# A decoder layer on one core: LN2's gain and bias rows made by TensorE transposes, a 1 MB weight load moved ahead, and one 4 MB piece loaded in two transfers instead of four

## The reference, cut to what matters

```python
h = layer_norm(ALPHA*h + hybrid_mixer(h, ...), ln1_g, ln1_b)
h = layer_norm(ALPHA*h + memory_cross_attention(h, mem_n, ...), ln2_g, ln2_b)     # LN2
# router: top 4 of 32 experts per token, softmax weights -> combine
for e in range(32):
    hid = clamped_swiglu(h @ w_mlp1[e] + b_mlp1[e])      # w_mlp1[e]: 1024 x 2048, 8 MB
    y   = y + combine[:, e:e+1] * (hid @ w_mlp2[e] + b_mlp2[e])   # w_mlp2[e]: 1024 x 1024, 4 MB
h = layer_norm(ALPHA*h + y, ln3_g, ln3_b)
```

## Time and profile before

| | |
|---|---|
| runs | 1135.2, 1135.61, 1135.63 us; median 1135.61 |
| profiled execution | 1137.09 us, of which the profiled span is 1135.2 us |
| busy in the span | PE 1084.9, PEld 522.0, DVE 322.2, ACT 228.6, POOL 8.1 us |
| transfers | 446.74 MB (here of 10^6 bytes) in all, mean 394 GB/s over the span |
| granted TensorE clock | mean 0.99 |

### The profile page before, as it was taken

The page is one execution under the profiler, slowest core; times in us unless marked ns, Lnnn a source line. Parts: engine busy times, 40 slices in busy tenths (PEclk is TensorE's granted clock), DMA queues, the critical chain, the costliest instruction groups (busy, mean ns, idle before and its releaser), DMA issues.

```text
span 1135.2 us, 15726 instructions
## 1 busy us (share of the span) xinstructions
PE 1084.9 (96%) x6536; PEld 522.0 (46%) x6536; DVE 322.2 (28%) x733; ACT 228.6 (20%) x411; POOL 8.1 (1%) x14
## 2 busy tenths in 40 slices
PE   9999999989999999999999999999999999999996
PEld 6888899843333333343333333333333333334331
DVE  6987775581111111121111111111111111012112
ACT  5667565440000100010010000000000000001001
POOL 0000000000000000000000000000000000000000
PEclk9999999999999999999999999999999999999999
DMA  9866868699999999999999999999999999999996
GB/s 354 295 193 238 289 209 331 230 388 419 436 431 435 432 433 432 435 433 433 432 434 434 432 435 433 433 432 435 433 432 433 434 434 431 431 430 429 432 426 250
DMA packets 41728, 446.74 MB, mean 394 GB/s; under 512 B 4832, under 2 KB 5728, under 8 KB 25088
## 3 DMA queue, kind: packets, MB, share of 16 engines
q1 hardware_dynamic: 41408, 445.76, 94.0%
q10 hardware_dynamic: 288, 0.52, 0.1%
HBM read 445.22 MB, written 1.05 MB: 393 GB/s over the span
## 4 chain that ended last, share of the span: by engine, by line
PE 58%; DMA 35%; SPq 3%; DVE 3%; issue 1%; ACT 0%; DVEq 0%
DMA ring<-in_w_mlp 33%; PE bank L1155 23%; PE bank L1199 9%; PE bank L685 5%; PE bank L687 5%; PE bank L686 5%; PE bank L1057 4%; PE bank L1045 2%; DMA w_raw<-in_w_in 2%; SPq L609 1%; PE bank L1094 1%; SPq L488 1%; SPq L502 1%; PE bank L927 1%; PE bank L911 1%; PE bank L1113 1%
## 5 line engine op out<-in xcount | busy, mean ns | idle before, releaser
L1155 PE MATMUL bank<-ring,live 128*64 128x512 f32 x2048 | 468.2, 605 | 27.9 <-DMA ring<-in_w_mlp 27.7
L1155 PEld LDWEIGHTS bank<-ring,live 128*64 128x64 f32 x2048 | 143.8, 138 | 310.4 <-issue 286.0
L1199 PE MATMUL bank<-ring,live 128*64 128x512 f32 x992 | 220.8, 596 | 6.8 <-DMA ring<-in_w_mlp 6.8
L1919 DVE COPY live<-bank 128x256 f32<-128x256 f32 x32 | 13.6, 425 | 527.8 <-PE bank L1087 527.8
L1199 PEld LDWEIGHTS bank<-ring,live 128*64 128x64 f32 x992 | 70.8, 137 | 130.8 <-issue 122.6
L1517 ACT ACTIVATE live<-bank 128x512 f32<-128x512 f32 x31 | 18.5, 597 | 325.1 <-PE bank L1094 325.1
L1589 DVE TENSOR_TENSOR w_low<-w_raw,w_high 128x1024 fp32r<-128x1024 f32 x61 | 72.3, 1221 | 23.8 <-ACT w_high L1291 23.6
L2009 DVE TENSOR_SCALAR live<-bank 128x256 f32<-128x256 f32 x64 | 24.2, 420 | 193.1 <-PE bank L1155 193.1
L1291 ACT ACTIVATE w_high<-w_raw 128x1024 fp32r<-128x1024 f32 x61 | 63.1, 1059 | 34.7 <-PE bank L687 16.6
L1513 ACT ACTIVATE live<-live 128x512 f32<-128x512 f32 x32 | 20.3, 635 | 239.4 <-DVE live L2009 239.4
L1045 PEld LDWEIGHTS bank<-pick,live 128*128 128x128 bf16 x1488 | 52.0, 118 | 27.0 <-issue 27.0
(11 more groups left out here) (253 smaller groups left out, 859.2 us busy)
## 6 DMA issues: line engine op xcount, KB each, us to landing
ring<-in_w_mlp SPq DMA_DIRECT2D x73, 4096.0 KB, 47.1
ring<-in_w_mlp SPq DMA_DIRECT2D x34, 2048.0 KB, 49.2
ring<-in_w_mlp SPq DMA_DIRECT2D x22, 1024.0 KB, 11.0
w_raw<-in_w_in SPq DMA_DIRECT2D x21, 512.0 KB, 10.0
w_raw<-in_w_mem_kv SPq DMA_DIRECT2D x16, 512.0 KB, 4.9
w_raw<-in_w_mix_out SPq DMA_DIRECT2D x8, 512.0 KB, 5.4
w_raw<-in_w_mem_q SPq DMA_DIRECT2D x8, 512.0 KB, 3.9
w_raw<-in_w_mem_o SPq DMA_DIRECT2D x8, 512.0 KB, 6.0
```

Of the source, the lines that this page charges most:

```text
L1155: mm = pe.matmul(up[j][64 * g:64 * g + SLOTS, :], x_e[:, k, :], columns(row, j, g), start=False, stop=(k == KC - 1))
L1199: mm = pe.matmul(to[64 * g:64 * g + SLOTS, :], stationary[:, P * c + 64 * u:P * c + 64 * u + SLOTS], slot(at)[:, col:col + 512], start=(u ...
```

## The change

LN2's rows are no longer loaded. TensorE makes them: `turn_gains(part, q)` turns a column of `token_cols`, broadcast over 128 columns, by four transposes of 128 x 128, which gives 512 of the 1024 gains (part 0) or biases (part 1) on all partitions, in a bank of PSUM. It is called four times inside `up_stage(1)`, after its steps k = 0, 1, 2 and 3. DVE's `normalise` is split: first all four multiplications (`scale_tokens`), the first two of which wait for the first call and the other two for the second, then all four additions (`shift_tokens`), in the order (tile 0, half 0), (0, 1), (1, 0), (1, 1), where half 0 waits for the third call and half 1 for the fourth. They read the rows from PSUM in an order of columns with steps of 128 (512 bytes) in the innermost four. The second operand was in SBUF before.

Place 21 is loaded at unit 56, where the rows were loaded, after the same wait. It is gone from its old place behind the quarters. The quarters become two loads of 2 MB, after `up_used` 1 and 2 (k = 1 and k = 3), and the waits on quarters in `up_stage(3)` become waits on halves.

```diff
 # SP
-                    sp.wait_ge(ln_ready, 12)          # place 21
+                    sp.wait_ge(ln_ready, 8)
                 if u == 56:
-                    sp.wait_ge(ln_ready, 8)
-                    load_gains(a["ln2_g"], a["ln2_b"])
+                    prefetch(21, 1)
-            for quarter, used, landed in ((0, first_used, parts_in[0]), (1, up_used, first_half_in[0]),
-                                          (2, first_used, parts_in[1]), (3, up_used, piece_in[0])):
-                sp.wait_ge(used, quarter // 2 + 1)
-                part = slice(2048 * quarter, 2048 * (quarter + 1))
-                sp.dma_start(slot(0)[:, part], expert_src(2, 0)[:, part]).then_inc(landed, 16)
-            prefetch(21, 1)
+            for half in range(2):
+                sp.wait_ge(up_used, half + 1)
+                load_half(2, 0, 0, half)
 # PE
+        gain_banks = [[banks[2], banks[6]], [banks[4], banks[5]]]
+            def turn_gains(part, q):
+                if part == 0 and q == 0:
+                    pe.wait_ge(token_cols_in, 16)
+                    pe.wait_ge(drained[2], bank_jobs[2])
+                    pe.wait_ge(drained[6], bank_jobs[6])
+                elif part == 1 and q == 0:
+                    pe.wait_ge(x_odd, KC // 2)
+                    pe.wait_ge(x_e_ready, 1)
+                for i in range(4):
+                    c = 4 * q + i
+                    mm = pe.transpose(gain_banks[part][q][:, P * i:P * (i + 1)],
+                                      token_cols[:, part, c:c + 1].broadcast_to([P, P]), ident)
+                mm.then_inc(gains_turned, 1)
                     if k % 2:
                         mm.then_inc(up_used if k < KC - 1 else up_done, 1)
-                    elif first and k < 4:
-                        mm.then_inc(first_used, 1)
+                    if first and k < 4:
+                        turn_gains(k // 2, k % 2)
 # DVE
-                x = h2[:, t, 512 * q:512 * (q + 1)]
-                step(dve.scalar_tensor_tensor(out=x, in0=x, scalar=ln_s[:, 4 + t, 1:2], in1=gb[:, 0, 512 * q:512 * (q + 1)],
+            def columns_of(t, q):
+                return h2[:, t, 512 * q:512 * (q + 1)].rearrange("p (m i) -> p m i", i=4)
+            def gain_rows(part, q):
+                dve.wait_ge(gains_turned, 2 * part + q + 1)
+                return gain_banks[part][q][:, :].rearrange("p (i m) -> p m i", i=4)
+            def scale_tokens(t, q):
+                x = columns_of(t, q)
+                step(dve.scalar_tensor_tensor(out=x, in0=x, scalar=ln_s[:, 4 + t, 1:2], in1=gain_rows(0, q),
                                               op0=ALU.mult, op1=ALU.mult))
-                dve.tensor_tensor(x, x, gb[:, 1, 512 * q:512 * (q + 1)], ALU.add).then_inc(ln_ready, 1)
+            def shift_tokens(t, q):
+                x = columns_of(t, q)
+                dve.tensor_tensor(x, x, gain_rows(1, q), ALU.add).then_inc(ln_ready, 1)
-            dve.wait_ge(gb_in, 96)
+            for q in range(2):
+                for t in range(NT):
+                    scale_tokens(t, q)
             for t in range(NT):
                 for q in range(2):
-                    normalise(t, q)
+                    shift_tokens(t, q)
```

More of the change, by code:

```diff
@@ L306, in decoder_layer @@
         minus_ready, centred, token_cols_in = sem("minus_ready"), sem("centred"), sem("token_cols_in")
-        early_in, first_used, parts_in = [sem(f"early_in{i}") for i in range(NHALF)], sem("first_used"), [sem(f"parts_in{i}") for i in range(2)]
+        early_in, parts_in = [sem(f"early_in{i}") for i in range(NHALF)], [sem(f"parts_in{i}") for i in range(2)]
         wt_ready, wt_turned, wtT_ready = sem("wt_ready"), sem("wt_turned"), sem("wtT_ready")
@@ L323, in decoder_layer @@
         before_last_half_in, last_half_in = ([sem(f"{name}{u}") for u in range(2)] for name in ("before_last_half_in", "last_half_in"))
-        last_up_in = sem("last_up_in")
+        last_up_in, gains_turned = sem("last_up_in"), sem("gains_turned")
         hot_ready, hot_used = sem("hot_ready"), sem("hot_used")
@@ L1104, in up_stage @@
             def up_stage(n, at, loads=None, first_loads=None, earlier=None, first=False, first_sum=False, weights=False, bias=False,
-                         tokens=False, scatter_first=False, early=False, quarters_in=None, seventh=None):
+                         tokens=False, scatter_first=False, early=False, seventh=None):
                 pe.wait_ge(hot_ready, n)
@@ L1134, in up_stage @@
                     else:
[L1135 to L1140, removed]
+                        if k % 4 == 0 and first_loads:
                             pe.wait_ge(first_half_in[at + k // 4], first_loads)
@@ L1186, in down_stage @@
                         if eighths is not None and 4 * u + c in (0, KC - 2):
-                            pe.wait_ge(eighths[u], 32)
+                            pe.wait_ge(eighths[u], 16)
                         if c == (1 if eighths is not None and u == 0 else 0) and halves[u] is not None:
@@ L1218, in _ @@
             down_stage(1, downs[0], None, ty, early=True)
-            up_stage(3, ups[0], 16, 16, earlier=(1, 2), first_sum=True, quarters_in=parts_in)
+            up_stage(3, ups[0], 16, 16, earlier=(1, 2), first_sum=True)
             gather_next(3)
@@ L1621, in apply_norm @@
                                              in1=gb[:, 1, halves[q]], op0=ALU.mult, op1=ALU.add).then_inc(ln_ready, 1)
-            def normalise(t, q):
-                x = h2[:, t, 512 * q:512 * (q + 1)]
-                step(dve.scalar_tensor_tensor(out=x, in0=x, scalar=ln_s[:, 4 + t, 1:2], in1=gb[:, 0, 512 * q:512 * (q + 1)],
+            def columns_of(t, q):
[6 more added lines that the diff above has]
+                step(dve.scalar_tensor_tensor(out=x, in0=x, scalar=ln_s[:, 4 + t, 1:2], in1=gain_rows(0, q),
                                               op0=ALU.mult, op1=ALU.mult))
-                dve.tensor_tensor(x, x, gb[:, 1, 512 * q:512 * (q + 1)], ALU.add).then_inc(ln_ready, 1)
+            def shift_tokens(t, q):
+                x = columns_of(t, q)
+                dve.tensor_tensor(x, x, gain_rows(1, q), ALU.add).then_inc(ln_ready, 1)
             def fixed_logits(t):
```

## The result

| | before | changed |
|---|---|---|
| median of 6 runs | 1135.27 us (1134.98 to 1135.63) | 1141.38 us (1139.84 to 1142.97) |
| ratio | | 1.0052, 95% interval 1.0039 to 1.0065 |
| profiled execution, span | 1137.09, 1135.2 | 1141.7, 1139.9 |

The change costs 6.1 us, 0.5%. The forecast of +1.7 had the sign but not the size, and the time lies outside the range.

What follows compares the result with a forecast made beforehand. The prediction took the weight stream at 433 GB/s as the bound. PE's lateness of 5.4 + 1.2 = 6.6 us, less a slack of 3.75 to 6.1, gave +1.7 us: 1135.61 + 1.7 = 1137.3 us, range 1134.2 to 1140.0.

Steps and rivals of the forecast that it cites:

- What bounds the kernel: Behind the front, one stream of weights at 433 GB/s bounds the kernel, and PE follows it.
- Part 1: Place 21 loaded at unit 56 costs zero; 1 MB less in the full stream gives -2.4 us.
- Part 2: Two 2 MB loads near 240 us: +0.4 us at most, counting only if nothing later opens a wider gap.
- Part 3: 16 transposes in the first up stage: 0.65 us per call, 2.6 for four; stage ends at 252.9.
- Part 4: LN2 waits for the transposes: everything behind it starts 5.4 us later, gather at 257.5, PE's pause 4.6 us.
- The rival of the slow reads: DVE pays for the 512-byte steps in PSUM, +2.1 us on three additions: 1139.4 us, chance 0.05.
- Part 5, the clock: PE's longer pause before the gather makes the granted clock fall: 1.2 us, bounds 0 and 1.7.
- The sum: PE 6.6 us late from the second expert on, less slack of 3.75 to 6.1 at 278.77 us: middle +1.7 us.
- the reading by landings: Slack at the 278.77 us load: it took 18.1 us to land, a lone one 12.0, so 6.1 us.
- the transposes overlap: Rival: transposes do not overlap among the matmuls, 16 take 4.8 us instead of 2.6; 1139.5 us, chance 0.03.
- The slower rival: At the 278.77 us issue: full 1.7 us of clock, slack only 3.75; +3.35 us, 1139.0 us, chance 0.28.
- by bytes: Slack at the 278.77 us load from bytes issued less moved: 5.15 us queued, less 1.4 for starting, 3.75 us.

Runs made afterwards that it cites:

- quarters_kept: The changed kernel with expert 2's first piece in four quarters again, place 21 still at unit 56; 1141.61 us against 1135.71, ratio 1.0047.
- moves_alone: The kernel before with only the load changes, no transposes, row loads left out (LN2 takes a constant column); 1133.42 us against 1135.66, ratio 0.9982.
- turns_alone: The changed kernel with the old loads (place 21 behind the quarters, four quarters), so only the transposes are new; 1140.91 us against 1135.66, ratio 1.0047.
- down_halves: The changed kernel with expert 2's w_mlp2, its first 4 MB load, in two halves of 2 MB; 1139.67 us against 1135.79, ratio 1.0035.
- late_: Five kernels: the kernel before plus 13, 24, 32, 43 or 63 constant transposes before the first gather; +0.1, +1.1, +1.8, +3.2, +5.5 us.
- the nine kernels of the table: The five late_* kernels, the changed kernel, that kernel with its pause filled by 26 transposes, turns_alone and quarters_kept; ratios 1.0004 to 1.0052 against the kernel before.
- late_63: The kernel before with 63 transposes of a constant on PE before the first gather; +5.5 us, ratio 1.0051.

## Why the prediction was right or wrong, point by point

- **What bounds the kernel**: right. The stream is at 431 to 434 GB/s from 310 to 1000 us in all kernels, the up stages of the changed kernel wait for the ring 13 times for 22.4 us between 560 and 1000 us (14 times, 25.8 before), and its loss was made before 310.
- **Part 1**: right. The load at unit 56 costs nothing that shows (the first up stage starts at 236.02 for 236.36), and the megabyte gives 2.2 us when it comes alone.
- **Part 2**: right that it doesn't count, as far as the intervals tell: quarters_kept equals the change, moves_alone gains almost all. The issues came at 240.44 and 245.34 (said: 240.7 and 245.4).
- **Part 3**: right: 0.65 us each, the up stage ends at 252.9 as forecast.
- **Part 4**: right, each number within 0.3 us. Last three additions from 245.92 (said 246.0), small steps 5.2 us late (5.4), gather at 257.29 (257.5), pause 4.39 (4.6). The additions took 0.68 us each and the multiplications 0.75, as before from SBUF (0.69 and 0.75), so the steps of 512 bytes in PSUM cost nothing. The rival of the slow reads falls.
- **Part 5, the clock**: right that it falls. In this execution it stood at 0.50 for 6.8 us and cost 1.8 where 1.2 was said, just outside the bounds of 0 to 1.7; in turns_alone and down_halves, after the same pause, it cost 1.0. SP's issue came 7.0 us later by the clock of the span and 7.4 by the start of the up stage; 6.6 was said.
- **The sum: this is the step that failed.** "The end moves by 6.6 less the slack", with a slack of 3.75 to 6.1 us. The forecast took the middle, 4.9. The slack is 1.5 (the late_* kernels). Of the 4.4 us by which the forecast fell short, up to 0.8 is the lateness, 3.4 the slack and 0.2 scatter. The rule itself (lateness less slack, one for one) held.
- Why the readings of the slack were too large. First, both asked how long the queue at 278.77 would last and took a load that is issued before it ends to follow without a loss. The trace of the changed kernel says no: the load of 295.31 went out 3.2 us before its forerunner landed (285.79 + 12.7 = 298.5), and the stream still ran at 334 GB/s for 5 us, 1.1 us lost; 286 to 289 lost 0.65 in the same way. The kernel before shows this already: 313 GB/s from 240 to 246 us, while four loads went out. The prediction saw that row, called it ragged and did not ask what it says of the slack.
- Second, the reading by landings, which was weighed equally and was the worse of the two, takes the last of a load's 16 completions. When the load of 278.77 went out, the one ahead had its last completion 8.5 us later but its first 4.9 us later. If each completion is one DMA engine's part (no run here shows that), one engine had 3.6 us less in its queue than the reading says. Nor is the lag of the last one a reserve: in the changed kernel first and last are 1.1 us apart for the load of 285.79 and 3.4 for the next, nearly the 3.6 of the kernel before.
- Third, both were read from one execution that was 1.8 us above the median. Against that same execution the nine kernels of the table give a slack of 2.0 to 3.7 us (lateness, less what the span grew by from the start of the first up stage), seven of them under 3. An execution whose stream is late against PE has a longer queue. So about 1 us of the missing slack is probably the choice of the execution; the kernel before was profiled once, so this is not shown.
- It was right that the saved megabyte is lost in the gap: turns_alone and late_63, which still load it, lie on one line with the changed kernel, which doesn't. In both turns_alone and the changed kernel the first completion of the second 4 MB load comes 64.6 us plus the lateness after the start of the first up stage.
- **Rivals**: the transposes overlap (falls: 0.65 for four, and 1.04 to 1.09 for eight). By the Trainium skill, page "TensorE: Matmul & The Clock Gate", section "Part 4: PE-mode transpose", one in bf16 takes 275 ns in a kernel. The prediction says that this trace disagrees, and that is a misreading: each of the 16 f32 ones here is recorded with 273 ns too (the median). They overlap, so that one follows the other after 0.11 to 0.16 us; only the sum that adds up single durations is refuted. The slower rival named the right place and direction, 1139.0, and was given 0.28, but its slack of 3.75 was too large as well; with the clock at its measured cost and the slack at 1.5 it is the result.
- **Chances**: 0.36 for slower was too low. The two readings of the slack differed by 2.35 us, more than the whole forecast; that alone said that it was not known.

Open: how the missing slack (3.75 by bytes, 1.5 measured) divides between the poor start of loads into a short queue, the first of the 16 parts that run dry, and the execution that it was read from. down_halves speaks for about 1.1 us at the first of the two 4 MB issues, within its interval.

## What to carry to other kernels

Where a transfer stream bounds the kernel, ask of each delay on the compute side how much is queued when its loads are let go, and measure that slack with a plain delay of 2, 4 and 6 us before trusting a number that is worked out from queued bytes, above all from one execution and from landings, which tell of the last part of a load alone. Small work that replaces a load belongs well ahead of what a second engine needs it for: the same 16 transposes cost 6 us between the first four steps and nothing that can be measured around the first one, because a second engine stood in order behind the last one. And a pause that grows may cost twice, once as time and once as clock.

## What the runs showed of the hardware that was not expected

- After a pause of 4.39 us the granted clock was 0.50 for 6.8 us (changed kernel, quarters_kept), after one of 4.40 us for 3.4 us (turns_alone, down_halves). After a pause of 2.25 us it was 0.50 for 3.4 us, after one of 2.03 it did not fall.
- Transposes alone held the clock: in late_63 PE did nothing else for 7.07 us, and the granted clock stayed at 1.00.
- f32 transposes of 128x128 in a row came every 0.11 us (43 in 4.88, 63 in 7.07), where four among other matmuls take 0.65 together.
- A 4 MB load issued 3.2 us before the queue's last one landed took 16.1 us, where 3.2 and 9.7 at 433 GB/s make 12.9. The one before it was issued 2.4 us before its forerunner landed and took 12.7, where the same sum gives 12.1.
- The 16 completions of a 4 MB load lay 3.6 us apart in the kernel before, and in the changed kernel 1.1 us for the first one after the queue had run dry and 3.4 for the next.
- A DVE operation whose operand in PSUM is read in steps of 512 bytes took 0.68 us for 128x512 (an addition), where the same one with the operand in SBUF took 0.69.
